# Overflow tiles placed between the experts' own tiles, with rings of their own; one-hot products as rounded part plus rest; one layer's modulation summed on DVE

## What is computed

```python
def gla_mixer(h, ...):                      # mixer of layer 2; layer 3 has lru_mixer
    proj = h @ w_in                         # 1024 x 3088
    ...
def grouped_moe(h, router_w, router_bias, w_gate, w_up, w_down):
    ...                                     # two experts of one group for each token
    for e in range(16):                     # d_model 1024, d_expert 512
        he = silu(t @ w_gate[e]) * (t @ w_up[e])
        out = out + combine[:, e:e + 1] * (he @ w_down[e])
    return out
...
sh1, sc1, g1, sh2, sc2, g2 = split(cond @ ada_w[i] + ada_b[i], 6)   # the modulation of a layer
x = x + g1 * mix
x = x + g2 * grouped_moe(modulate(rmsnorm(x), sh2, sc2), ...)
```

## Time and profile before

| | |
|---|---|
| median of the runs, us | 2803.23 (2800.44 to 2810.59) |
| the profiled execution: its own time, us | 2816.16 |
| its span, us | 2814.4 |
| PE busy / DVE / ACT / POOL, share of the span | 86% / 42% / 22% / 23% |
| read and written by DMA | 934 MB, mean 332 GB/s |
| expert part of layer 2 (first step to last `add`) | 1974.84 to about 2290.6 us |
| mixer of layer 2, projection slots | 1744.11 to 1867.40 us |

### The profile page before, as it was taken

How to read it: one execution, slowest core, us unless ns; L and a number is a source line. 1 busy time by engine, 2 the same in 40 slices (tenths; PEclk the granted TensorE clock), 3 DMA queues, 4 the chain that set the end, 5 groups by cost and what they waited for, 6 DMA issues and landing times.

```text
span 2814.4 us, 26206 instructions
## 1 busy us (share of the span) xinstructions
PE 2422.6 (86%) x9674; PEld 1281.0 (46%) x9676; DVE 1169.7 (42%) x2825; ACT 625.0 (22%) x1780; POOL 644.9 (23%) x823
## 2 busy tenths in 40 slices
PE   6999888787778989977787788987999988799998
PEld 2577433333333567433333334346454456544544
DVE  0326666766664336667766763023100022320001
ACT  1112323322233122323332333111110022110101
POOL 1103433333332102433343331100222000012100
PEclk7989998899999999999899899987999999799999
DMA  8748999999997757999999997853899135579970
GB/s 328 301 171 332 416 421 422 421 422 421 421 422 314 286 207 312 417 422 421 422 421 422 421 421 328 312 204 135 359 421 421 70 135 201 247 307 421 421 299 16
DMA packets 130128, 934.40 MB, mean 332 GB/s; under 512 B 14288, under 2 KB 16336, under 8 KB 16592
## 3 DMA queue, kind: packets, MB, share of 16 engines
q0 software_dynamic: 114768, 835.96, 72.1%
q1 hardware_dynamic: 15232, 96.75, 8.8%
HBM read 1070.02 MB, written 1.05 MB: 381 GB/s over the span
## 4 chain that ended last, share of the span: by engine, by line
PE 54%; DMA 26%; DVE 15%; ACT 4%; issue 1%; SPq 0%; DVEq 0%; ACTq 0%
PE units L1101 15%; PE units L645 13%; DMA arena<-rows,idx 11%; PE accs L887 11%; DMA wide<-rows,idx 8%; DMA ring<-stream 5%; PE units L1079 3%; PE accs L1146 3%; DVE wide L1804 3%; DVE arena L1804 2%; PE units L660 2%; PE accs L725 2%; DMA wide<-experts 2%; ACT arena L1331 1%; DMA arena<-ada 1%
## 5 line engine op out<-in xcount | busy, mean ns | idle before, releaser
L887 PE MATMUL accs<-wide,arena 128*128 128x512 f32 x1040 | 518.7, 654 | 146.7 <-ACT arena L1331 144.9
L887 PE MATMUL accs<-arena 128*128 128x512 f32 x1008 | 482.7, 633 | 93.2 <-ACT arena L1331 93.2
L887 PEld LDWEIGHTS accs<-wide,arena 128*128 128x128 f32 x1040 | 211.3, 208 | 438.2 <-issue 254.3
L555 POOL DMA_INDIRECT wide<-rows,idx x260 | 245.0, 942 | 602.1 <-PE accs L887 422.0
L1101 PE MATMUL units<-wide,arena 128*64 128x512 f32 (+1 forms) x1728 | 368.1, 597 | 8.4 <-DMA wide<-experts 6.0
L887 PEld LDWEIGHTS accs<-arena 128*128 128x128 f32 x1008 | 203.1, 205 | 369.9 <-issue 248.8
L1199 ACT ACTIVATE arena<-units 128x512 f32<-128x512 f32 (+2 forms) x204 | 111.2, 559 | 1017.0 <-PE units L645 312.7
L645 PE MATMUL units<-arena,ring 128*128 128x256 f32 (+1 forms) x1344 | 300.2, 386 | 28.3 <-ACT arena L1226 14.0
L555 POOL DMA_INDIRECT arena<-rows,idx x252 | 237.3, 942 | 359.9 <-PE accs L887 322.1
L645 PEld LDWEIGHTS units<-arena,ring 128*128 128x128 f32 x1344 | 256.3, 200 | 74.2 <-issue 38.6
L1101 PE MATMUL units<-arena 128*64 128x512 f32 (+1 forms) x960 | 232.7, 593 | 0.5 <-ACT arena L1199 0.5
(11 more groups left out here) (301 smaller groups left out, 2102.1 us busy)
## 6 DMA issues: line engine op xcount, KB each, us to landing
wide<-experts POOLq DMA_DIRECT2D x123, 1024.0 KB, 13.4
wide<-experts SPq DMA_DIRECT2D x93, 1024.0 KB
wide<-ada POOLq DMA_DIRECT2D x88, 1024.0 KB, 9.2
arena<-experts POOLq DMA_DIRECT2D x69, 1024.0 KB, 16.2
ring<-stream SPq DMA_DIRECT2D x62, 1024.0 KB, 6.8
arena<-experts SPq DMA_DIRECT2D x51, 1024.0 KB
arena<-side SPq DMA_DIRECT2D x8, 1024.0 KB, 8.2
wide<-ada SPq DMA_DIRECT2D x7, 1024.0 KB, 16.9
```

Source lines behind the costliest of these rows:

```text
L555: pool.indirect_dma_start(row_slot(i), None, rows[l], bass.IndirectOffsetOnAxis(ap=idx[:, n, k:k + 1], axis=0)).then_inc(row_sem(i), 16)
L887: ins = mm(o[:, half * 512:(half + 1) * 512], diag[:, i % (2 * GROUP), :], row_slot(PICKS * l + i)[:, D + half * 512:D + (half + 1) * 512] ...
```

## The change

- **Order of tiles.** `ORDER = (0, 1, 8, 2, 3, 4, 9, 5, 6, 7, 10)`: the overflow tiles 8, 9 and 10 stand at places 3, 7 and 11.
- **Rings.** The own loads have a ring of 7 slots (`OWN_RING`). Block 0 of each overflow tile has a ring of 2 slots (`LANE_RING`), blocks 1, 2 and 3 have one slot each.
- **One-hot products.** `to`, `bT`, the tokens and the outputs are kept as float32r, a rounded 32-bit type. The tokens and the outputs are split: ACT writes the rounded part (`tok_hi`, `o_hi`), POOL the rest of the tokens (`tok_lo`), DVE the rest of the outputs (`o_lo`). `place` and `add` do one float32r product for the part and one for the rest. `place` now serves two tiles at once (256 columns, 32 products), every second tile. The transposed one-hot `bT` comes from two float32r products with an identity, and the combine weight of each place from two float32 products with a column of ones; DVE multiplies it into the hidden vector.
- **Modulation in layer 2.** DVE multiplies each of the 24 pieces (128x2048) by its column of the condition and adds them up in `ada_sums`, 8 pieces for each of three sums; PE then sums over partitions with 4 products for each sum (`sum_added`), in the midst and at the end of its slots. The modulation ring has 6 slots instead of 7, in all layers.

```diff
-ADA_RING = 7
+ADA_RING = 6
-MOE = dict(to=8192, back=11008, tok=16384, hs=18432, si=19456, act=19968, aT=20480, bT=20992, o=21504)
-EXP_AT = SLOT_AT[0:7] + SLOT_AT[10:14]
+OWN_RING, LANE_RING = 7, 2
+EXP_AT = SLOT_AT[0:OWN_RING] + (("keys", 0),) + SLOT_AT[10:14]
+ORDER = (0, 1, 8, 2, 3, 4, 9, 5, 6, 7, 10)
+def place_of(l, i):
+    if i < OWN:
+        n = (l - DEPTH) * OWN + i
+        return n % OWN_RING, n // OWN_RING
+    n, lane = divmod((l - DEPTH) * EXTRA + i - OWN, 4)
+    if lane == 0:
+        return OWN_RING + n % LANE_RING, n // LANE_RING
+    return OWN_RING + LANE_RING + lane - 1, n
...
                         for k in range(4):
                             for b in range(TB):
-                                ins = mm(bank(u)[:, k * P:(k + 1) * P], tok[:, b, ...], to[:, b, p * P:(p + 1) * P], ...)
+                                for part, tok in enumerate(toks):
+                                    ins = mm(bank(u)[:, j * T:(j + 1) * T], tok[:, b, k * P:(k + 1) * P],
+                                             to[:, b, at:at + 2 * P], start=b + part == 0, stop=b + part == TB)
+                def turn_back(p):
+                    for b in range(TB):
+                        mm(bank(u)[:, b * P:(b + 1) * P], to[:, b, p * P:(p + 1) * P], ident_r[:, :], ...)
+                    for b in range(TB):
+                        ins = mm(bank(u)[:, T:T + 1], back[:, b, p * P:(p + 1) * P], one[:, :], ...)
...                     # add
-                        ins = mm(acc[d // 2][...], o[:, d * P:(d + 1) * P], bT, ...)
+                        for part, o in enumerate(os):
+                            ins = mm(acc[d // 2][...], o[:, d * P:(d + 1) * P], bT, ...)
...                     # the order of the blocks in a step: block 0 last
+                    order = [(j + 1) % len(loads) for j in range(len(loads))]
...                     # gla on PE
-                for c in range(2):
-                    token_slots(SLOT_OF["gv", l] + 2 * c, UNIT_OF["gv", l] + 2 * c, hT, adas=2)
+                for c in range(2):
+                    token_slots(SLOT_OF["gv", l] + 2 * c, UNIT_OF["gv", l] + 2 * c, hT)
+                    sum_added(l, c)
...                     # DVE, for each piece
+                w = cact[:, which // DEPTH, k:k + 1]
+                if k == 0:
+                    ts(ada_sums, ada_piece(i), w, None, ALU.mult).then_inc(ada_added, 1)
+                else:
+                    stt(ada_sums, ada_piece(i), w, ada_sums, ALU.mult, ALU.add).then_inc(ada_added, 1)
...                     # DVE, for each tile: the rest of the output
-                        took(v.tensor_copy(o[:, c * 512:(c + 1) * 512], bank(u)[:, :]), u)
+                        took(tt(o_lo[:, cut], bank(u)[:, :], o_hi[:, cut].bitcast(F32), ALU.subtract), u)
```

More of the change, by code:

```diff
@@ L66, with _tile_plan, take @@
 SIDE = (2, 3, 4, 5)
+BATCHES = (TILES + 1) // 2
+def _tile_plan():
+    n = 0
+    at = [{} for _ in range(TILES)]
+    batch = []
+    def take(k):
+        nonlocal n
+        n += k
+        return tuple(range(n - k, n))
+    batch.append(take(4))
+    at[0]["back"], = take(1)
+    for p in range(TILES):
+        (at[p]["gate"],), (at[p]["up"],), (at[p]["turn"],) = take(1), take(1), take(1)
+        if p % 2 and p + 1 < TILES:
+            batch.append(take(4))
+        if p + 1 < TILES:
+            at[p + 1]["back"], = take(1)
+        at[p]["down"] = take(2)
+    return at, batch, n
+TILE_AT, BATCH_AT, TILE_UNITS = _tile_plan()
 def plan():
@@ L1860, in gla @@
                 tt(zz, zz, e, ALU.subtract).then_inc(la_ready, 1)
+                for j in (1, 2):
+                    for k in range(KT):
+                        add_piece(l, j, k)
                 gs = room(L2["gs"], TB * GH, GDV)
@@ new lines, in of_run @@
+                def of_run(a, b, run):
+                    e, n, _ = run
+                    return spread(a[:, 16 * b + e:16 * b + e + n], 2, [P, n, CAP])
+                made = len(RUNS) * TB * (l - DEPTH)
+                for part in (RUNS[:1], RUNS[1:]):
+                    for run in part:
+                        for b in range(TB):
+                            tt(by_expert(to, b, run), count[:, 0:CAP].unsqueeze(1).broadcast_to([P, run[1], CAP]),
+                               of_run(place, b, run), ALU.is_equal).then_inc(spread_ready, 1)
+                    made += TB * len(part)
+                    dve.wait_ge(spread_ready, made)
+                    for run in part:
+                        for b in range(TB):
+                            last = run == part[-1] and b == TB - 1
+                            if last:
+                                steps.sync()
+                            ins = tt(by_expert(back, b, run), by_expert(to, b, run).bitcast(F32),
+                                     of_run(comb, b, run), ALU.mult)
+                            if last:
+                                ins.then_inc(back_ready, 1)
+                            else:
+                                steps(ins)
```

280 lines of the change are left out of this document (185 added, 95 removed).

## The result

The changed kernel takes 2856.74 us (median of 4 runs, 2851.43 to 2861.85) where the kernel before, on the same chip, takes 2806.54 (4 runs, 2800.44 to 2810.59). The ratio is 1.0171, 95% interval 1.0144 to 1.0197: slower by 50 us. The forecast was 2823, slower by 20. The sign held, and so did the wide range of 2780 to 2868; the range that the forecast gave its own case, 2805 to 2842, did not, and the loss is two and a half times the one forecast.

What follows compares the result with a forecast made beforehand. PE was taken to set the end of the expert parts. Terms of +2, +25, -10 and +3 gave +20 on the profiled 2816.2, so 2836, or 2823 us for the median; range 2805 to 2842.

Steps and rivals of the forecast that it cites:

- The sign: Whole kernel: slower at 51%, faster at 25%, no change (under 0.5%, 14 us) at 24%.
- the wide range of 2780 to 2868: Whole kernel: the median in us, meant to hold for 8 in 10.
- its own case: Whole kernel: the summed terms, median 2823 us (+0.7%), range 2805 to 2842, given 45%.
- PE's tile: Expert parts: a tile's work on PE falls from 28.5 to 23.8 us, at 0.11 us a float32r record.
- The own ring: Expert parts: with 7 slots, PE waits for own loads from the second tile on, 19.8 us a layer.
- Unused blocks: Overflow tiles without used blocks: single slots make four steps a tile wait 1.16 us, 13.9 us a layer.
- The rival by which unused loads count late: Overflow tiles: an unused load's semaphore comes some 1.7 us later in 20 steps, +34 us, 2857; chance 13%.
- Layer 2 in sum: Expert part of layer 2: shorter PE work plus ring waits, 317.5 us against 315.8, +2.
- Layer 3: Expert part of layer 3: tile 8's two used blocks add waits and a lowered clock, +25 us in all.
- Mixer: Mixer of layer 2: 24 pieces leave PE, less a 5.7 us wait at the second sum and other losses, -10 us.
- Ring of modulation pieces: Modulation loads: one slot fewer costs 1.5 us in each of two bursts, +3 us.
- Before the first tile: Ahead of the expert tiles: smaller one-hot matrices, ACT takes and POOL's subtraction beside the ranking, counted as 0.

## Why the forecast was right in sign and wrong in size

*PE's tile.* Forecast 23.8 us with `add` at 1.8 and `place` at 3.5; measured 2.02 and 3.91. The record was taken at 0.11 us and is 0.122 to 0.126. For 11 tiles and the 5 places between steps this is 2.4 + 2.0 us a layer. The last wait, 1.58 for 0.98, adds 0.6. By the Trainium skill's page "FP8 and Floating Point Precision" (TensorE Precision Notes) true float32 takes four passes, and reduced float32 has its operands cut to 22 bits; that the latter is one pass is read out of this, the page does not say it. The trace has 0.122 against twice 0.22, 0.28 rather than 0.25, so it agrees nearly with one against four.

*The own ring: the step that failed.* The forecast had 14 waits, 19.8 us (the waits that it lists add up to 20.1). The trace of layer 2 has 20, 24.8 us in brackets. Where the bracket is 1.31 the wait costs what lies between 4.97 from start to start and the pace of 3.44, which is 1.53, so 0.2 more for each. In all some 29 us, 9 more in a layer. The first wait comes at the fifth step of the first tile, not in the second tile. Two inputs were off. The first is the time from a slot's read to the bytes. After the change the first step ends at 1952.33:

```profile
1952.88 1.11 POOL L641 DMA_DIRECT2D wide<-experts  x2 [18.01 <-PE units L1231]
```

```profile
1953.00:1954.00 1.00, 1.00 (x6) 0.29 (x4) 0.96 (x3) 0.00 (x0) 0.99 (x2) 1.00 0.00 0
1954.00:1955.00 1.00, 1.00 (x8) 0.34 (x6) 0.93 (x3) 0.00 (x0) 0.00 (x0) 1.00 0.84 188
```

188 of 421 GB/s in the slice from 1954 means bytes from about 1954.55: 2.2 us. The same reading of the earlier trace rows, 172 of 421 from 1980, gives 1980.6 and 2.3 us, where the forecast took 1.8: the row was there and was misread. The second is in the code (`held`, `release`), before the change too: where a step is the last of a unit (a bank of PSUM), one of its slots is given free only by the first product that follows, of the next step or of `add`. So it stays taken while PE waits for the next loads or does transposes. And the edit changed it in a way that the forecast did not see: with block 0 last in a step, the slot held back is that of the step's first load instead of its last, and as POOL issues in order, both next loads wait for it (before, the two went out at 1989.09 and 1995.44, one by one). The first tile's fourth step ends at about 1962.7, the fifth starts at 1965.78, and only after that POOL issues the next two:

```profile
1967.12 1.05 POOL L641 DMA_DIRECT2D wide<-experts  x2 [6.33 <-PE units L1231]
```

With both, and the measured records and waits, the load-by-load replay gives 323 us for the part from the first step to the last `add`, the figure that the expectations above start from. The measured counterpart is 329.6, so some 6 us are not explained by it. That the number of slots within reach is the cause is shown (6 own slots: +12.4; the same 12 shared: own waits down to 18.3, all the blocks' waits gone). How the 9 us divide between the later bytes and the held slot, and what its new place costs, was not tried.

*Unused blocks.* Forecast 1.16 us in four steps, 13.9 a layer; measured 1.11 to 1.17 in brackets, once 1.46, exactly there, 13.9 in sum, and 15.7 from start to start. The mechanism held, and leaving two tiles' loads out gave 12.5 us back in layer 2. The rival by which unused loads count late gave 2857, the time that was measured, and was still wrong: its mark was a wait of about 3 us, and no such wait is at an unused block; the load counted 0.18 us after its issue. The time alone would have confirmed it.

*Layer 2 in sum:* +2 forecast, +16.0 measured. The 14 us between are 9 from the own ring, 2 from the blocks, 5 from records and the end. That makes 16; the 2 too many were not traced to anything.

*Layer 3.* Beyond the 14 us that it shares with layer 2, it is 9 us over the forecast. Tile 8's waits were 27.6 (22.5 forecast), its slow steps cost some 11 us over 3.44 each (12 forecast); against layer 2 the tile is longer by 33.4, forecast 29.9. One by one, the tile's waits were to be 6.5, 4.7, 4.9, 1.5 and 4.9 and are 9.35, 5.31, 5.06, 2.25 and 5.60; more than half of the miss is the first, during which DMA moves 425 GB/s from 2530 to 2542, block loads and own loads together. The own waits are 29.7 for 24.8, where +1.5 was forecast, and a step behind one of 3.10 took 5.35 us for 3.65. This leaves about 1 of the 9 open. The Trainium skill's page "DMA: Bandwidth & Descriptors" (Anatomy of one DMA), which the forecast set beside its 4.7 us for "every transfer", gives its 2.0 us for loads that GpSimd issues. SP issues the block loads, and what they took is in these rows. The mechanism held, and without the block loads the layer equals layer 2.

*Mixer.* Forecast -10, measured -11.3, and +11.5 when undone. The wait at the second sum was to be 5.7 and is 4.75 (timeline of PE):

```profile
1806.01 1.44 PE L841 MATMUL accs<-wide,one 128*32 128x512 f32 x8 [4.75 <-DVE wide L1686]
```

*Ring of modulation pieces.* +3 forecast. PE's waits for `wide<-ada`, 19.5 us in 13 places before, are 21.5 in 15; this can't be told from none.

*Before the first tile.* Counted at 0, and this wait is wrong by 3.4 us a layer: PE's wait for the router was 3.26 us before and is 6.62. The row of before, beside the one of 6.62 above:

```profile
1963.43 0.61 PE L1058 MATMUL units<-tf,before 128*128 128x16 f32 x2 [3.26 <-DVE psr L2051]
```

It was seen that POOL's subtraction runs beside the ranking, but not that it would hold DVE up. The Trainium skill's page "SBUF — State Buffer" (SBUF: two separate sides) has that rule: GpSimd and VectorE share a pair of ports, and of a GpSimd operation and a VectorE operation in a 2-port mode or with two inputs in SBUF, whichever starts first has it for its whole instruction. The trace agrees, since DVE's operations end with GpSimd's. The stretches as a whole still became shorter (-2.4 and -1.8): the wait before the first `place` fell from 3.15 to 1.37 us in each layer, and in layer 2 one of 2.49 for the projection ring is gone.

The sum of the terms was +20. Without the stretch ahead of the mixer the trace has +48.7, of which layer 2 is 14 over and layer 3 23 over, less some 8 by which the other stretches are under. The likeliest case had the right mechanisms, with most terms of the expert parts too small, and the time lies outside its range. The sign was no strong call: the forecast gave slower 51%. Both layers share the own ring, so its error counts twice, and the range of "15 to 25 a layer" for it was too narrow.

## What to carry to other kernels

A ring that is cut up by kind of load has, for each kind, only the depth of its own part, and the part that is idle lends nothing. Here the same 12 slots in one ring, in the order of use, turned +50 us into -18 with the order and the records unchanged. What weaving can bring is bounded by the ring: in an overflow tile of 29.5 us the 7 own slots took 17 us of loads (7 x 2.49) and then DMA stood idle. To count slots times the time of a load against the length of the gap is a reading of this, not a rule that the runs tested. The weave paid with the divided rings (26 us in the medians) and not measurably with the shared one. And where a wait ends each step, take its price from start to start: here a bracket of 1.31 cost 1.53.

## What the runs showed of the hardware

- A float32r record of 256 columns took 0.122 to 0.126 us, where a float32 record of 256 columns took 0.22, both at a granted clock of 1.00.
- Two DVE operations of 128x4 took 2.41 us for 0.36, until the end of a GpSimd subtraction of 128x512 (1.24 us each). On DVE the same four subtractions took 2.49 us in all, on GpSimd 4.95.
- An unused load lets the waiting step start 1.31 us later than its pace, with the issues of three blocks in turn inside; PE started 0.18 us after the last of them.
- From a slot's read to the first bytes of its next load POOL's queue needed 2.2 to 2.3 us.
